# Forgetting attention: transposed value products on two column sets, denominators from ScalarE

## The reference

```python
def fox_prompt(q, k, v, logf):
    cum = jnp.cumsum(logf, axis=1).transpose(0, 2, 1)
    def block(i):
        s = jnp.einsum('bqhe,bkhe->bhqk', qb, k) * SCALE
        s = s + cq[..., :, None] - cum[:, :, None, :]
        s = jnp.where((t0 + jnp.arange(Q_BLOCK))[:, None] >= kpos[None, :], s, NEG_INF)
        return jnp.einsum('bhqk,bkhe->bqhe', jax.nn.softmax(s, axis=-1), vf)
```

## Time and profile before

| quantity | us |
|---|---|
| median of the three executions shown | 3129.94 |
| the three executions | 3137.76, 3129.54, 3129.94 |
| span of the profiled execution, first to last instruction | 3133.8 |
| part of it from the first turned scores of slot 1 to the last value product (626 to 1041) | 415 |

### The profile page before, as it was taken

One profiled execution on the slowest core, in us unless ns is written; L12 is line 12 of the kernel. 1 busy time (PEld: TensorE's weight loads), 2 busy tenths in 40 slices (PEclk: granted clock), 3 DMA queues, 4 the chain that ended last, 5 costly groups with the idle time before them and its releaser, 6 DMA issues. The chain is left out here.

```text
span 3133.8 us, 45320 instructions
## 1 busy us (share of the span) xinstructions
PE 2985.0 (95%) x16457; PEld 2560.7 (82%) x16457; DVE 1613.1 (51%) x2998; ACT 870.3 (28%) x1670; POOL 746.9 (24%) x512
## 2 busy tenths in 40 slices
PE   8999999989999899979979999999999999999997
PEld 5888889867676799867769999999997788888886
DVE  5113210267687588856645555445556544444445
ACT  4223321233332456533332111122214111111112
POOL 4002100134443254522202221111222211122210
PEclk9999999999999899989989999999999999999999
DMA  4455335567674343358651111111113311111101
GB/s 150 166 202 182 116 133 159 144 193 200 200 213 128 105 124 104 80 145 242 207 216 62 41 40 40 55 66 41 41 54 121 136 52 40 41 50 58 54 14 55
DMA packets 237384, 350.26 MB, mean 112 GB/s; under 512 B 75337, under 2 KB 172138, under 8 KB 231263
## 3 DMA queue, kind: packets, MB, share of 16 engines
q1 hardware_dynamic: 236295, 325.80, 33.6%
q0 software_dynamic: 944, 22.61, 1.9%
HBM read 283.53 MB, written 93.97 MB: 120 GB/s over the span
## 5 line engine op out<-in xcount | busy, mean ns | idle before, releaser
L2639 POOL TENSOR_TENSOR cm_dn_lo<-cm_dn_raw,cm_dn_hi 128x1024 fp32r<-128x1024 f32 x44 | 108.3, 2483 | 974.0 <-ACT cm_dn_hi L2688 974.0
L3376 PE MATMUL pj_acc<-pj_w_hi,pj_h_hi 128*128 128x480 f32 (+3 forms) x896 | 335.2, 374 | 0.9 <-DVE pj_h_lo L3251 0.9
L3377 PE MATMUL pj_acc<-pj_w_lo,pj_h_hi 128*128 128x480 f32 (+3 forms) x896 | 333.4, 372 | 0.0
L3378 PE MATMUL pj_acc<-pj_w_hi,pj_h_lo 128*128 128x480 f32 (+3 forms) x896 | 333.1, 372 | 0.0
L2932 PE MATMUL cm_g_ps<-cm_h_hi,cm_up_hi 128*128 128x344 f32 (+1 forms) x880 | 310.1, 352 | 11.6 <-DVE cm_h_lo L2744 11.2
L2934 PE MATMUL cm_g_ps<-cm_h_hi,cm_up_lo 128*128 128x344 f32 (+1 forms) x880 | 308.5, 351 | 0.0
L2932 PE MATMUL cm_u_ps<-cm_h_hi,cm_up_hi 128*128 128x344 f32 (+1 forms) x880 | 308.2, 350 | 0.0
L2934 PE MATMUL cm_u_ps<-cm_h_hi,cm_up_lo 128*128 128x344 f32 (+1 forms) x880 | 307.8, 350 | 0.0
L2933 PE MATMUL cm_g_ps<-cm_h_lo,cm_up_hi 128*128 128x344 f32 (+1 forms) x880 | 307.7, 350 | 0.0
L2933 PE MATMUL cm_u_ps<-cm_h_lo,cm_up_hi 128*128 128x344 f32 (+1 forms) x880 | 307.0, 349 | 0.0
L3257 DVE TENSOR_TENSOR pj_w_lo<-area,pj_w_hi 128x480 fp32r<-128x480 f32 (+3 forms) x112 | 75.6, 697 | 381.5 <-ACT pj_w_hi L3213 381.4
(11 more groups left out here) (448 smaller groups left out, 6472.0 us busy)
## 6 DMA issues: line engine op xcount, KB each, us to landing
area<-in_w_up SPq DMA_DIRECT2D x44, 1024.0 KB, 7.2
fp_kv_low<-in_fox_kv SPq DMA_DIRECT2D x168, 256.0 KB, 3.0
area<-in_fox_kv SPq DMA_DIRECT2D x88, 256.0 KB, 3.0
cm_dn_raw<-in_w_down SPq DMA_DIRECT2D x44, 512.0 KB
out_s_win<-in_cache POOLq DMA_DIRECT2D x8, 2047.0 KB, 9.0
proj_a<-area SPq DMA_DIRECT2D x48, 240.0 KB
sp_raw<-proj_b SPq DMA_DIRECT2D x16, 640.0 KB, 4.0
area<-in_w_a SPq DMA_DIRECT2D x10, 960.0 KB, 7.2
```

The lines of the kernel that those rows point to most:

```text
L2639: pool.tensor_tensor(dn_lo[:, s], dn_raw[:, s], dn_hi[:, s].bitcast(F32), ALU.subtract).then_inc(dn_ready, 1)
L3376: pe.matmul(out, h_hi[:, k, place(t)], w_hi[:, j % 2, k, 0:wide], start=(k == 0), stop=False)
L3377: pe.matmul(out, h_hi[:, k, place(t)], w_lo[:, j % 2, k, 0:wide], start=False, stop=False)
L3378: last = pe.matmul(out, h_lo[:, k, place(t)], w_hi[:, j % 2, k, 0:wide], start=False, stop=(k == KT - 1))
```

## The change

- `value` swaps its operands: 64 columns of values (`v_tok`) are stationary, up to 512 columns of `probs` move. Even key tiles write partitions 0 to 63 of `o_ps`, odd ones 64 to 127, so that two column sets of TensorE are used. It works in groups of four key tiles and stands further behind; `probs` has six buffers.
- The column of ones is gone. ScalarE's `exp_sum` goes over every score tile in `s_ps`, in place, with that piece's own maximum as bias, and adds the row up into `den`. `exp_scale` makes the factors from a piece's maximum to the block's, and VectorE's `denominators` joins them. Score number `u` now waits for `summed`, not `maxed`.
- The result lies transposed: ScalarE's `copy_o` takes it out of `o_ps`, TensorE's `turn_o` transposes it into `z_ps`, and `normalise` adds the two halves and divides. It moves from slot 1 to slot 3 of the next block, the store from slot 3 to 5.
- The maximum is stored negated, which drops one small VectorE operation from `m_tok`'s chain. The constants are loaded once for this and the next stage.

```diff
+        self.v_tok = sb("v_tok", [P, 2, TILES, HD])
...
+    GROUP, PROBS = 4, 6
+    first_group = [f // GROUP for f in first]
...
+            if i == 3 and b > 0:
+                z_uses.append(("o", b - 1))
...
-        probs = sb("probs", [P, 3, QB])
-        mx = sb("mx", [P, 2, 4, 4])
+        probs = sb("probs", [P, PROBS, QB])
+        neg = sb("neg", [P, 2, 4, 4])
+        den = sb("den", [P, 2, 4, 4])
+        scale = sb("scale", [P, 2, 4, 4])
...
+        oT = sb("oT", [P, QB])
...
-                    if i == 3 and b > 0:
+                    if i == min(5, size[b] - 1) and b > 0:
...
-                last = v.reduce_max(mx[:, b % 2, j, k:k + 1], s_ps[:, (first[b] + n) % 2, 0:w], AX.X)
+                last = v.reduce_max(neg[:, b % 2, j, k:k + 1], s_ps[:, (first[b] + n) % 2, 0:w], AX.X, negate=True)
...
-                    dve.link(v, v.reduce_max(top[:, b % 2], mx[:, b % 2, :, 0:q + 1], AX.X))
-                    dve.link(v, v.tensor_scalar(top[:, b % 2], top[:, b % 2], -1.0, None, ALU.mult))
+                    dve.link(v, v.tensor_reduce(top[:, b % 2], neg[:, b % 2, :, 0:q + 1], AX.X, ALU.min))
...
+                    v.tensor_tensor(scale[:, b % 2, :, 0:q + 1], top[:, b % 2].unsqueeze(2).to_broadcast([P, 4, q + 1]),
+                                    neg[:, b % 2, :, 0:q + 1], ALU.subtract).then_inc(scale_in, 1)
+
+            def denominators(b):
+                q = blocks[b][1]
+                v.wait_ge(summed, first[b + 1])
+                v.wait_ge(scale_ready, b + 1)
+                dve.link(v, v.tensor_tensor(scale[:, b % 2, :, 0:q + 1], scale[:, b % 2, :, 0:q + 1],
+                                            den[:, b % 2, :, 0:q + 1], ALU.mult))
+                dve.link(v, v.reduce_sum(rden[:, b % 2], scale[:, b % 2, :, 0:q + 1], AX.X))
+                dve.link(v, v.reciprocal(rden[:, b % 2], rden[:, b % 2]))
 
             def normalise(b):
-                o = o_ps[:, 0:4 * (HD + 1)].rearrange("p (j e) -> p j e", e=HD + 1)
-                v.wait_ge(valued, first[b + 1])
-                dve.link(v, v.reciprocal(rden[:, b % 2], o[:, :, HD]))
+                z, o = z_ps[:].rearrange("p (j a e) -> p j a e", a=2, e=HD), o_tok[:, b % 2]
+                j = 1 if blocks[b][1] == 0 else 0
+                v.wait_ge(o_turned, b + 1)
                 if b >= 2:
                     v.wait_ge(stored[b % 2], 16 * (b // 2))
-                v.tensor_tensor(o_tok[:, b % 2], o[:, :, 0:HD], rden[:, b % 2].unsqueeze(2).to_broadcast([P, 4, HD]),
+                if j:
+                    v.tensor_copy(o[:, 0], z[:, 0, 0])
+                dve.link(v, v.tensor_copy(o[:, j:], z[:, j:, 0]))
+                v.tensor_tensor(o[:, j:], o[:, j:], z[:, j:, 1], ALU.add).then_inc(o_joined, 1)
+                v.wait_ge(o_joined, b + 1)
+                v.tensor_tensor(o, o, rden[:, b % 2].unsqueeze(2).to_broadcast([P, 4, HD]),
                                 ALU.mult).then_inc(o_ready, 1)
 
...
-                    if i == 1 and b > 0:
-                        normalise(b - 1)
+                    if i == 1:
+                        denominators(b)
                     for part in parts_at.get((b, i), []):
                         low(*part)
+                    if i == 3 and b > 0:
+                        normalise(b - 1)
...
-                if u >= 3:
-                    act.wait_ge(valued, u - 2)
-                act.activation(probs[:, u % 3, 0:w], t_ps[:, u % 2, 0:w], ACT.Exp).then_inc(exped, 1)
+                if u >= PROBS:
+                    act.wait_ge(valued, (u - PROBS) // GROUP + 1)
+                act.activation(probs[:, u % PROBS, 0:w], t_ps[:, u % 2, 0:w], ACT.Exp).then_inc(exped, 1)
+
+            def exp_sum(b, n):
+                q, (j, k), u = blocks[b][1], tiles_in[b][n], first[b] + n
+                s = s_ps[:, u % 2, 0:QB if k < q else (j + 1) * P]
+                act.wait_ge(maxed, u + 1)
+                act.activation(s, s, ACT.Exp, bias=neg[:, b % 2, j, k:k + 1],
+                               accum_out=den[:, b % 2, j, k:k + 1]).then_inc(summed, 1)
+
+            def exp_scale(b):
+                at = scale[:, b % 2, :, 0:blocks[b][1] + 1]
+                act.wait_ge(scale_in, b + 1)
+                act.activation(at, at, ACT.Exp).then_inc(scale_ready, 1)
+
+            def copy_o(b):
+                act.wait_ge(valued, first_group[b + 1])
+                if b:
+                    act.wait_ge(o_turned, b)
+                act.activation(oT[:], o_ps[:], ACT.Copy).then_inc(o_copied, 1)
...
+                    if i == 2 and b > 0:
+                        copy_o(b - 1)
                     exp(b, i)
                     for part in parts_at.get((b, i), []):
                         high(*part)
+                    for n in scores_at.get((b, i), []):
+                        exp_sum(b + 1, n)
                 if b + 1 < NBLK:
                     shift(b + 1)
+                    exp_scale(b + 1)
...
-                    pe.wait_ge(maxed, u - 1)
+                    pe.wait_ge(summed, u - 1)
...
-            def value(b, i):
-                (h, q), u = blocks[b], first[b] + i
-                diag = max(0, i - 4 * q)
-                pe.wait_ge(exped, u + 1)
-                if i == 0:
+            def value(b, g):
+                (h, q), u = blocks[b], first[b] + GROUP * g
+                pe.wait_ge(exped, u + GROUP)
+                if g == 0:
                     pe.wait_ge(v_landed, 16 * (h + 1))
                     pe.wait_ge(part_hi, part_no["a", 0, 1])
                     if b:
-                        pe.wait_ge(o_ready, b)
-                for j in range(diag, 4):
-                    last = pe.matmul(o_ps[:, j * (HD + 1):(j + 1) * (HD + 1)],
-                                     probs[:, u % 3, (j - diag) * P:(j - diag + 1) * P], v_one[:, h % 2, i],
-                                     start=(i == 0 and j == 0), stop=(i == 4 * q + j and j == 3))
+                        pe.wait_ge(o_copied, b)
+                for k in range(GROUP):
+                    i, at = GROUP * g + k, (k % 2) * HD
+                    lo = max(0, i - 4 * q) * P
+                    last = pe.matmul(o_ps[at:at + HD, lo:QB], v_tok[:, h % 2, i], probs[:, (u + k) % PROBS, 0:QB - lo],
+                                     start=(i < 2), stop=(i >= size[b] - 2))
                 last.then_inc(valued, 1)
+
+            def turn_o(b):
+                z_wait(("o", b))
+                pe.wait_ge(o_copied, b + 1)
+                for j in range(4):
+                    last = pe.transpose(z_ps[:, j * P:(j + 1) * P], oT[:, j * P:(j + 1) * P], ident)
+                last.then_inc(o_turned, 1)
...
-                    if i >= 2:
-                        value(b, i - 2)
+                    if i % GROUP == 1 and i > 1:
+                        value(b, i // GROUP - 1)
+                    if i == 1 and b > 0:
+                        value(b - 1, size[b - 1] // GROUP - 1)
                     for p in parts_at.get((b, i), []):
                         part(*p)
+                    if i == 3 and b > 0:
+                        turn_o(b - 1)
                 if b + 1 < NBLK:
                     turn_max(b + 1)
-                for i in range(size[b] - 2, size[b]):
-                    value(b, i)
+            value(NBLK - 1, size[NBLK - 1] // GROUP - 1)
+            turn_o(NBLK - 1)
```

50 lines of the change are left out of this document (29 added, 21 removed).

## The result

The changed kernel takes 3175.09 us, the median of 4 runs (3173.64 to 3184.2), against 3133.02 (3129.54 to 3137.76) for the kernel before: a ratio of 1.0145, 95% interval 1.012 to 1.017. It is slower by 42 us. The forecast was 3168, between 3126 and 3212.

A forecast was written before the change was run, and what follows sets the result against it. TensorE, busy 380 of the stage's 415 us, was taken as the bound, with score slots then looping through ScalarE. 39 + 18 - 17 - 6 - 8 + 8 + 3 = +37, say +38, on 3129.94 gave 3168, range 3126 to 3212.

The forecast's parts named there:

- The circle: Score slots: scores wait for ScalarE's sums, looping through TensorE and ScalarE; 3.31 us (3.04 to 3.70) against 2.63.
- Score steps in all: 66 steps between slots with scores: +39 us from the longer loop, +18 from other delays.
- the +18: Score slots: ScalarE's copies, decode exponentials, decode coinciding with value groups, and late VectorE maxima add 18 us.
- Plain steps: 46 steps without scores: cheaper value products save 0.38 us each, -17 us.
- Part steps: 32 part slots: half the value saving, as transposes through `z_ps` take nearly as long as TensorE's work; -6 us.
- Block changes: Value tail leaves 16 changes, 0.5 us each, -8; waits for `turn_o` and VectorE passes in eight blocks, +8.
- The end: First four scores' sums and, at the end, group, copy, transpose and joining: +3 us.
- The tiling drain: Value groups: changing tiling mode twice for each of 40 groups, priced 80 x 0.16 = 13 us, mostly in TensorE's waits.
- Nothing on balance: Rival: score slots stay at 2.63 us, only savings are left, 3110 us; chance 0.10.
- Column sets don't overlap: Rival: value products on two column sets run in series, plain and part slots gain nothing, 3227 us; chance 0.06.
- The clock: Rival: idle TensorE drops to 1.2 GHz in a third of score and plain steps, about 3196 us; chance 0.12.

The follow-up runs named there:

- sums_only: Kernel before, with ScalarE's sums over the score tiles added and scores waiting for them, values as before: 3177.65 us, ratio 1.0153.
- half_sums: Changed kernel with each of ScalarE's sums over scores taken over the first half of its columns only: 3159.27 us, ratio 1.0094.
- turned_first: Changed kernel with the turned score issued ahead of the slot's two scores on TensorE, except in a block's first slot: 3144.23 us, ratio 1.0044.
- no_sums: Changed kernel without ScalarE's sums over score tiles, denominators made from ones, scores waiting for maxima alone: 3127.21 us, ratio 0.9985.
- one_set: Changed kernel with all value products on the first column set, in partitions 0 to 63: 3223.22 us, ratio 1.0291.
- sums_first: Changed kernel with ScalarE's sums over a slot's two scores put before the exponential of its turned scores: 3158.14 us, ratio 1.008.
- turned_pairs: The turned_first kernel with value products in groups of two key tiles instead of four: 3140.35 us, ratio 1.0028.

## Why the prediction was right

**The circle.** The decisive step held. Predicted 3.31 us against 2.63, or 0.59 per step with narrow pieces; the slot is 3.22, sums_only has it without the values, and half_sums and turned_first change it by their dose and by the order. Term by term, from the timeline above, the exponential was 0.50 for 0.55, the first sum 0.66 for 0.72, the second with its read 0.78 for 0.81, the hand-over 0.05 for 0.10, and the score was longer, 0.57 for 0.47. ScalarE is busy 241 us in the stage where I said 270. The sums' lengths by form in the changed kernel (count, busy us, mean ns), to the earlier trace rows:

```profile
L781 ACT ACTIVATE fp_s<-fp_s,fp_neg 128x512 f32<-128x512 f32 x112 | 73.7, 658 | 1.2 <-DVE fp_neg L680 1.1
...
L781 ACT ACTIVATION_READ_ACCUMULATOR fp_s<-fp_s,fp_neg 128x1 f32 x160 | 32.6, 204 | 0.1
```

**Score steps in all** were forecast at +39 and +18 and are +62.6. The mean step of 3.57 lies 0.35 above the steady 3.22, which is the +18's part (23). How this divides between ScalarE's copies, late maxima and the clock wasn't measured; 2.7 us of it are the first block's first step alone (5.95).

**Plain steps**, forecast -17, gave -9.4. The saving per full tile was 0.32 (0.81 to 0.49), not 0.38, and I charged it to all 46 steps, many of which hold the narrow tiles of the diagonal. With wide tiles, in the last block, the four slots up to 1066.40 (0.55, 0.86, 0.57, and 2.44 with the group) take 1.1 each, near the 1.0 of the forecast, and 1.47 in sums_only.

**Part steps**, forecast -6, gave -7.0 in the table, but 7 of that is before's clock. I counted 32 slots with transposes, and the last head has none. Its eight steps took 11.7 us against 14.7 in sums_only, 3 less; the 24 with transposes took 61.5 against before's 58.6, 3 more. There the saving is gone: TensorE waits 5.7 us in them for the `z_ps` chain (L852 for L672), 4.9 before, and 2.0 for the bank before `turn_o`.

**Block changes**, forecast -8 and +8 for tails and chain, gave -10.9. But no_sums, with the same tails and chain, has -0.9, close to the forecast's zero, and sums_only, with neither, has -4.5. So most of the gain comes with the longer score slots and not from the tails; by what way no run shows.

**The end.** From the last turned score to the next stage's first product it took 9.9 us (1038.27 to 1048.21) and takes 12.6 (1073.53 to 1086.10), +2.6 for the +3.

**The sum.** That +38 met +42 is in part luck. The circle's size was right, but its steps cost 6 more than forecast and the plain steps gained 8 less, the block changes gained 11 more for a reason that I did not have, and the part steps' -7 is before's clock.

**The tiling drain.** The rule of the Trainium skill that changing the tiling mode drains TensorE (TensorEngine Tiling, Key Properties) was priced at 13 us. A full group costs 1.97 where the columns alone would give an estimated 4 x 0.43 = 1.7: 0.27 at both ends together, 11 us if all 40 groups have it. So the trace agrees in size, but no run here divides it between a drain and the wait of the group's first load. The Trainium skill's other rule, that loads overlap a running product only if the row groups differ (TensorE: Matmul & The Clock Gate, Part 3), isn't borne out: eight matmuls with their loads take 1.94 us, where the columns' 1.7 and eight loads of 0.11 in series would be 2.6. (The 34 groups that I gave this rule are 24 wide ones and 16 narrow ones counted by their columns; every one of the 40 has eight loads.)

**Rivals.** "Nothing on balance" needed a circle of 2.6 and failed with it. "Column sets don't overlap" is excluded by one_set: 3.58 against 1.87, and 48 us in the time. "The clock" came partly. Two stretches of the changed kernel, and its stage at 0.91 against 0.94:

```profile
626.00:634.00 8.00, 5.96 (x24) 4.48 (x22) 2.48 (x6) 5.09 (x13) 3.71 (x2) 0.50 0.82 276
762.00:770.00 8.00, 6.64 (x16) 4.25 (x18) 4.10 (x12) 2.96 (x8) 2.92 (x2) 0.50 0.93 185
```

Both are busy only part of the time and at 0.50, the 1.2 GHz level. But before had such stretches too, and sums_only and turned_first have them: the difference of the means, 0.03 of 448 us, is 13 us of TensorE's time at most, much of it spent waiting anyway.

**What the forecast didn't see** is that little is left without the circle. I valued the change without it at 3110, and no_sums has 3127. VectorE's additions and the four-tile bursts are worth some 13 us each there in the medians (8.5 and 7.0 in the stage ends). Why the score steps stay at 2.7 whatever is taken away is open; VectorE's 2.5 us in a slot with a gather is the nearest reading. It cost nothing in the forecast, since the circle covered it.

## What to carry to other kernels

- Before adding a reader to a double-buffered tile, write the loop through both engines in the order of their queues, as a sum. Here it is exponential, sum, sum, score, turned score: 3.22 us against 2.63, and it was right to a tenth. If it is too long, look for a call that can move ahead of the waiting one: one moved call gave back 31 of 42 us.
- Removing work from the busiest engine need not pay by its own length: 0.3 us less per score step gave nothing here (178.6 us against 173.3). Read the other engines' work per slot, not their share of the stage (VectorE has 68% of the stage, but all of a score slot with a gather).
- The same products in smaller bursts may be worth more: groups of two instead of four gave 13.5 us without the sums, and 4, within the spread, with them.

## What the hardware showed that I had not expected

A VectorE instruction on four columns took up to 7.5 us beside GpSimd's products. In turned_first (timeline):

```profile
623.96 4.51 POOL L454 TENSOR_TENSOR area<-fp_q_own,area 128x2048 f32<-128x2048 f32 x1
623.97 6.82 DVE L690 TENSOR_TENSOR fp_m_tok<-fp_top,fp_m_tok 128x4 fp32r<-128x4 f32 x1
...
628.41 2.34 POOL L461 TENSOR_TENSOR fp_prod<-fp_kv_low,fp_q_own 128x1024 f32<-128x1024 f32 x1
...
630.94 1.01 PE L919 MATMUL fp_z<-sp_consts,fp_m_tok 128*4 128x128 f32 x4 [8.39 <-DVE fp_m_tok L690]
```

L690 has 16 executions with a median of 0.17 us; this one started 0.01 after a GpSimd product and ended (630.79) just after the next one's end (630.75). TensorE stood 8.39 us for it, and the first turned score came at 633.46 instead of 624.43. In the changed kernel the same operation started at 621.60, 1.25 us ahead of the GpSimd product, and took 0.17. So a shift of a microsecond or two at the stage's start seems to cost 9. sums_first and turned_pairs show the same late start (633.61, 633.25), there by the operation before it: the cast of L689, 0.34 us in the changed kernel, takes 7.26 and 7.48. It also bears on the small operation that the change drops from the maximum's chain. By line (count, busy us, mean ns), before and after:

```profile
L676 DVE TENSOR_SCALAR fp_top<-fp_top 128x4 f32<-128x4 f32 x16 | 7.2, 450 | 0.6
...
L681 DVE CAST fp_m_tok<-fp_top 128x4 fp32r<-128x4 f32 x16 | 2.7, 171 | 0.5
```

```profile
L689 DVE CAST fp_m_tok<-fp_top 128x4 fp32r<-128x4 f32 x16 | 8.4, 523 | 0.6
```

L676 is gone, but the operation behind it, L689 for L681, now takes three times as long: 9.9 us for the two became 8.4 for one. What is held up seems to be whatever small operation comes next while GpSimd's product runs (the reduction just before, L684, keeps its 0.16); the rows show the coincidence in time, and no run here took GpSimd's work away.
